# Handover from the up to the down projection: load order, glu stores, h in quarters, and turn 1's sums

## The reference, cut to what matters

```
h = x + hybrid_mixer(rms_norm(x, norm1_w), ...)
u = causal_dwconv(rms_norm(h, norm2_w) @ w_up, conv_w) + conv_b      # w_up: 1024 x 5632, 3 taps
gate, val = split(u, 2)
x = h + (silu(gate) * val) @ w_down                                  # w_down: 2816 x 1024
out = rms_norm(x, final_norm_w)
```

## Time and profile before

| | |
|---|---|
| median of 3 runs | 1639.51 us (1639.09 to 1640.14) |
| the profiled execution | 1641.98 us |
| its span | 1640.3 us, mean granted TensorE clock 0.993 |
| busy: TensorE matmul, VectorE, ScalarE, GpSimd | 1596.2, 882.6, 578.5, 648.6 us |
| TensorE's share of the chain that ended last | 91% |
| up projection from turn 1 | about 998 to 1408 us |
| down projection and final norm | about 1409 us to the end |

### The profile page before, as it was taken

The page is one execution under the profiler, slowest core; times in us unless marked ns, Lnnn a source line. Parts: engine busy times, 40 slices in busy tenths (PEclk is TensorE's granted clock), DMA queues, the critical chain, the costliest instruction groups (busy, mean ns, idle before and its releaser), DMA issues.

```text
span 1640.3 us, 20502 instructions
## 1 busy us (share of the span) xinstructions
PE 1596.2 (97%) x7955; PEld 1328.8 (81%) x7955; DVE 882.6 (54%) x1326; ACT 578.5 (35%) x838; POOL 648.6 (40%) x477
## 2 busy tenths in 40 slices
PE   7999999999999999999999998999999999889998
PEld 4888888888888888887888886888888888678886
DVE  5322223454536353567453248566665566678876
ACT  4422222123232234323222234444444444344445
POOL 3334332213132222224324357878888877000011
PEclk9999999999999999999999999999999999999999
DMA  5232432121213042444466022222333332696685
GB/s 170 70 97 79 122 89 60 42 72 34 69 38 86 20 125 76 129 109 140 141 209 224 37 93 71 90 91 92 111 112 116 104 103 78 206 336 207 196 265 183
DMA packets 202764, 192.24 MB, mean 117 GB/s; under 512 B 23236, under 2 KB 156844, under 8 KB 202668
## 3 DMA queue, kind: packets, MB, share of 16 engines
q1 hardware_dynamic: 202448, 190.85, 37.4%
q10 hardware_dynamic: 220, 0.09, 0.0%
HBM read 142.57 MB, written 48.33 MB: 116 GB/s over the span
## 4 chain that ended last, share of the span: by engine, by line
PE 91%; DVE 5%; DMA 2%; issue 1%; SPq 1%; ACT 0%; POOL 0%; DVEq 0%
PE acc L561 37%; PE acc L2449 12%; PE bank_ab L1407 7%; PE bank_ab L2449 6%; PE acc L2459 6%; PE att_ps L2449 5%; PE att_ps L2459 3%; PE bank_ab L2459 3%; PE acc L1842 3%; PE att_ps L1482 2%; PE bank_ab L1842 1%; PE att_ps L1842 1%; DMA f_raw<-in_w_down_dram 1%; PE att_ps L1464 1%; DVE u_t_full L1798 1%
## 5 line engine op out<-in xcount | busy, mean ns | idle before, releaser
L561 PE MATMUL acc<-xh,w_high 128*128 128x512 f32 x832 | 276.8, 409 | 0.6 <-POOL xl L1731 0.6
L561 PE MATMUL acc<-xl,w_high 128*128 128x512 f32 x832 | 262.2, 392 | 0.0
L561 PE MATMUL acc<-xh,w_low 128*128 128x512 f32 x832 | 261.1, 390 | 0.0
L972 POOL TENSOR_TENSOR w_low<-w_raw,w_high 128x1024 fp32r<-128x1024 f32 x49 | 117.4, 2396 | 347.3 <-ACT w_high L1054 347.3
L561 PEld LDWEIGHTS acc<-xh,w_low 128*128 128x128 f32 x832 | 156.5, 188 | 34.2
L561 PEld LDWEIGHTS acc<-xl,w_high 128*128 128x128 f32 x832 | 156.6, 188 | 33.9
L561 PEld LDWEIGHTS acc<-xh,w_high 128*128 128x128 f32 x832 | 147.1, 189 | 27.0 <-issue 3.8
L1145 ACT ACTIVATE sc<-sc,mx 128x128 f32<-128x128 f32 (+1 forms) x96 | 35.5, 440 | 173.5 <-DVE mx L1351 173.5
L1245 DVE SCALAR_TENSOR_TENSOR cs<-acc,prm,cs 128x1023 f32<-128x1023 f32 (+2 forms) x36 | 46.1, 1281 | 77.0 <-ACT cs L1072 76.1
L2236 POOL TENSOR_TENSOR f_h<-f_h,f_fw 128x512 f32<-128x512 f32 x8 | 11.0, 1369 | 184.8 <-ACT f_junk L2159 184.8
L2459 PE MATMUL acc<-f_w_high,f_gh 128*128 128x512 f32 x176 | 69.9, 397 | 12.2 <-DVE f_gl L2321 12.1
(11 more groups left out here) (386 smaller groups left out, 3831.6 us busy)
## 6 DMA issues: line engine op xcount, KB each, us to landing
w_raw<-in_w_in_dram SPq DMA_DIRECT2D x51, 512.0 KB, 4.5
f_raw<-glu_d SPq DMA_DIRECT2D x66, 256.0 KB, 3.0
f_raw<-in_w_down_dram SPq DMA_DIRECT2D x55, 256.0 KB, 3.8
w_raw<-in_w_up_dram SPq DMA_DIRECT2D x24, 512.0 KB, 5.1
glu_d<-u_free_high SPq DMA_DIRECT2D x22, 512.0 KB, 4.7
u_raw_even<-in_w_up_dram SPq DMA_DIRECT2D x20, 512.0 KB, 4.6
f_raw<-gsum_d SPq DMA_DIRECT2D x33, 256.0 KB, 3.3
conv_d<-so SPq DMA_DIRECT2D x16, 512.0 KB, 3.0
```

What stands on the lines that cost most here:

```text
L561: mm = nc.tensor.matmul(out[:, lo:hi], w, xx[:, lo:hi], start=first and j == 0, stop=last and j == 2)
L972: g.tensor_tensor(wl[:, n % 2], raw[:, n % 2], wh[:, n % 2].bitcast(F32), ALU.subtract).then_inc(s_wlo, 1)
```

## The change

- Room 0 of `f_raw` now lies where the even turns' raw weights lay (8 KB into the old room), so load 0 is issued in SP's pass for turn 20, behind that turn's `load_back`; `combine(0)`, whose target lies over a moving operand of turn 21, waits for turn 21's second product. Room 3 is cut into three pieces 8 KB apart; rooms 1 and 2 keep a piece of the old room each.
- The last glu store and glu sum store are issued behind load 12 in place of ahead of load 8.
- h is loaded in 16 quarters (4 row tiles by one 512-column half at a time, 256 KB each), one with each of steps 9 to 24, in place of 8 tiles of 512 KB with steps 8 to 15. Each `add` to a quarter waits for that quarter's four loads (the semaphores `rows_loaded`, which the first norm used for x, count on). `final_norm_w` follows at step 25 in place of 16.
- VectorE's turn 1 runs mix 0, 1, 2, `taps(0, 0)`, mix 3, `taps(0, 1)`, mix 4, `gated(0)`, mix 5, `glu_sum(0)`; before it ran `taps(0, 0)`, mix 0, `taps(0, 1)`, `gated(0)`, mix 1 to 3, `glu_sum(0)`, mix 4, mix 5.

```diff
@@ ffn: rooms @@
-    room = nc.alloc_sbuf_tensor_at("f_raw", [P, RING, 3, HALF], F32, offset=OL_AT)
+    slots = [nc.alloc_sbuf_tensor_at(f"f_raw{j}", [P, 3, HALF], F32, offset=at)
+             for j, at in enumerate((OL_AT + 8 * KB, OL_AT, OL_AT + 16 * KB))]
+    slots.append(nc.alloc_sbuf_tensor_at("f_raw3", [P, 3, 4 * HALF], F32, offset=OL_AT + 6 * KB))
...
     def slot(n):
-        return room[:, n % RING]
+        return slots[n % RING][:, :, 0:HALF]
@@ ffn: SP @@
                 if t >= KH:
                     load_back(t)
+                if t == LAST - 1:
+                    load(0)
 
             sp.wait_ge(s_prod, NP * (LAST - 1) + 3)
-            for n in range(NS):
-                if n == 2 * RING:
+            for n in range(1, NS):
+                load(n)
+                if n == KH + 1:
                     store_glu(LAST)
                     store_sum(LAST)
-                load(n)
-                if n == 2 * RING:
+                if n == KH - 2:
 
                     sp.wait_ge(s_prod, NP * LAST)
                     sp.wait_ge(s_mix, NP * LAST)
-                if 2 * RING <= n < 2 * RING + NT:
-                    st = n - 2 * RING
-                    sp.dma_start(h[st], halves(h_d[st * P:(st + 1) * P, :])).then_inc(s_h, 16)
-                if n == 2 * RING + NT:
+                if KH - 2 <= n < KH - 2 + 2 * NT:
+                    quarter, i = divmod(n - KH + 2, NTH)
+                    rows = slice((NTH * (quarter // 2) + i) * P, (NTH * (quarter // 2) + i + 1) * P)
+                    cols = slice(quarter % 2 * HALF, (quarter % 2 + 1) * HALF)
+                    sp.dma_start(result(i, HQ[quarter]), h_d[rows, cols]).then_inc(s_rows[quarter], 16)
+                if n == KH - 2 + 2 * NT:
@@ ffn: VectorE, combine @@
                     loaded(dve, n)
+                    if n == 0:
+
+                        dve.wait_ge(s_prod, NP * (LAST - 1) + 2)
@@ ffn: VectorE, add @@
                     to = result(i, name)
+                    if name in HQ:
+                        dve.wait_ge(s_rows[HQ.index(name)], 16 + 16 * NTH)
@@ ffn: VectorE, turns @@
             for t in range(1, FT):
-                if t > 1:
-                    mix(t - 1, 6)
+                if t == 1:
+
+                    for n in range(3):
+                        mix(t, n)
+                    taps(t - 1, 0)
+                    mix(t, 3)
+                    taps(t - 1, 1)
+                    mix(t, 4)
+                    gated(t - 1)
+                    mix(t, 5)
+                    glu_sum(t - 1)
+                    continue
+                mix(t - 1, 6)
                 taps(t - 1, 0)
-                if t == 1:
-                    mix(t, 0)
                 taps(t - 1, 1)
-                if t > 1:
-                    mix(t, 0)
+                mix(t, 0)
                 gated(t - 1)
...
                 if p and RING <= kk < RING + NTH:
-                    if p == 1 and kk == RING:
-                        dve.wait_ge(s_h, 16 * NT)
                     add(p - 1, kk - RING)
```

More of the change, by code:

```diff
@@ L240, in build @@
         m_ring, g_ring, u_ring = (ring_sems(phase) for phase in "mgu")
+        s_rows = [sem(f"rows_loaded{i}") for i in range(NT)]
         ups = UpRoom(nc, sem, xh, xh_at, xl, xl_at, ring, u_ring[0], nc.sbuf_base)
@@ L243, in build @@
               norm1_w, norm2_w, dn_conv_w, ffn_conv_w, ffn_conv_b, w_in2, dn_a_log, dn_dt_bias, dn_onorm_w, conv_d, og_d, ob_d, gate_d, m_d, t_d,
-              w_pa2, w_pb2, ring, m_ring, g_ring)
+              w_pa2, w_pb2, ring, m_ring, g_ring, s_rows)
         merged, merged_banks = merge_and_project(nc, sem, acc, every, ident, small, prm, xh, xl, w_pa2, w_pb2, w_o2, places, ready,
@@ L247, in build @@
         ffn(nc, sem, sb, mixed, merged, merged_banks, acc, bank_ab, att_ps, every, prm, small, xh, xl, w_up2, w_dn2, h_d, glu_d, gsum_d, final_norm_w,
-            outd, ring, u_ring, xl_at, ups)
+            outd, ring, u_ring, xl_at, ups, s_rows)
 class UpRoom:
@@ L385, in norm_head @@
 def norm_head(nc, sem, xd, norm1_w, norm2_w, dn_conv_w, ffn_conv_w, ffn_conv_b, ident, ones, prm, small,
-              xs, xn, junk, n1w, stage, tps, prm_ps, acc, xh, xl, w_in2, ring, m_ring):
+              xs, xn, junk, n1w, stage, tps, prm_ps, acc, xh, xl, w_in2, ring, m_ring, s_x):
     ss, ms, rstd, mhalf = small[:, 0:8], small[:, 8:16], small[:, 16:24], small[:, 24:32]
@@ L391, in norm_head @@
     first_cols = [job[2] for job in mixer_jobs()[0:2]]
-    s_x = [sem(f"n_x_loaded{i}") for i in range(NT)]
     s_par, s_n1w = sem("n_params_loaded"), sem("n_weight_loaded")
@@ L577, in mixer @@
           norm1_w, norm2_w, dn_conv_w, ffn_conv_w, ffn_conv_b, w_in2, dn_a_log, dn_dt_bias, dn_onorm_w, conv_d, og_d, ob_d, gate_d, m_d, t_d,
-          w_pa2, w_pb2, ring, m_ring, g_ring):
+          w_pa2, w_pb2, ring, m_ring, g_ring, s_rows):
     bank_a, bank_b = bank_ab[:, 0:HALF], bank_ab[:, HALF:S]
@@ L736, in mixer @@
             xs, xn, vt[:], n1w, stage, [att_ps[:, :], bank_ab[:, :]], acc[1][:, HALF:HALF + PT_COLS], acc,
-            xh, xl, w_in2, ring, m_ring)
+            xh, xl, w_in2, ring, m_ring, s_rows)
         A4 = bank_a[:, :].rearrange("p (h c) -> p h c", h=NH)
@@ L1918, in ffn @@
 def ffn(nc, sem, sb, mixed, merged, merged_banks, acc, bank_ab, att_ps, every, prm, small, xh, xl, w_up2, w_dn2, h_d, glu_d, gsum_d, final_norm_w,
-        outd, ring, u_ring, xl_at, ups):
+        outd, ring, u_ring, xl_at, ups, s_rows):
     raw, wh, wl = ring
@@ L1953, in ffn @@
     s_k, s_bank, s_sum = sem("f_k_done"), sem("f_bank_done"), sem("f_summed")
-    s_h, s_fw = sem("f_h_loaded"), sem("f_norm_loaded")
+    s_fw = sem("f_norm_loaded")
+    HQ = ("00", "01", "10", "11")
     s_sq, s_ms, s_rstd = sem("f_squares"), sem("f_mean_square"), sem("f_rstd")
```

## The result

The changed kernel takes 1626.64 us (median of 6 runs, 1624.81 to 1627.56) against 1639.6 us of 6 runs of the kernel before: 13.0 us less, ratio 0.9921, 95% interval 0.9908 to 0.9934. The profiled execution took 1627.18 us, its span is 1625.4 us, 14.9 less than before. Forecast were 1621.5 and a gain of 18.0: the time lies in the range, 5 us above the point.

What follows compares the result with a forecast made beforehand. TensorE was taken to carry the chain, so only its waits and low-clock time could be won. Handover 12.8 (15.7 less 0.7, 1.0, 1.2) plus turn 1 5.2 gave 18.0, off the median 1639.51: 1621.5 us, range 1617.0 to 1627.5.

Steps and rivals of the forecast that it cites:

- Part 1: Turn 1's sums ahead of turn 0's taps: 6.77 us late becomes a 1.6 wait for GpSimd, gain 5.2 (4.2 to 6.1).
- Part 2: Load 0 issued a turn earlier: load 1 lands at 1405.1, down projection starts without its 1.66 us gap.
- Part 3: VectorE's chain after combine 1: load 5's 2.16 us wait dropped, taps at 1416.0 on before's clock, step 6 loses 0.7.
- Part 4: Glu store later: loads 8 to 12 no longer queue behind it, the 8.1 us wait goes, step 7 loses 1.0.
- Part 5: New VectorE wait: combine 11 waits for both last stores, landing taken as 3.9 us, step 10 loses 1.2.
- Part 6: h in quarters with steps 9 to 24: same 4 MB, 16 issues, cost nothing, hidden under the steps.
- The starved case: Rival in the down projection: h transfers starve the sixteen steps from step 9, time 1644 us, chance 0.03.
- I take the 18.0 off the median: Whole kernel: the 18.0 us gain is subtracted from the runs' median of 1639.51, giving 1621.5.
- clock full throughout: Sign of being right, listed with turn 1's: TensorE's granted clock stays full; 0.50 in either place would show it wrong.
- no new waits: Rival, turn 1 and handover: faster loads, stores in 3.1, GpSimd undisturbed; at most 22.5 us gained, 1617.0, chance 0.15.
- the store wait's rival: At step 10 the store wait replaces the load wait: 5.0 + 2.1 in place of 1.2, 1627.4 us, chance 0.12.
- the others: Rivals: early load does nothing, 1623.8, chance 0.12; turn 1 stays slow, 1625, 0.08; transfers starve the steps, 1644, 0.03.

Runs made afterwards that it cites:

- a0: The changed kernel again, no edit, profiled and timed beside the kernel before; ratio 0.9926, span 1623.1 us.
- e4: The changed kernel with load 0 issued in its old place, behind the wait for turn 21's third product; ratio to before 0.9941.
- e5: The changed kernel with the quarters of h loaded with steps 13 to 28 in place of 9 to 24; ratio to before 0.9925.
- e6: The kernel before with only the last glu store and sum store moved behind load 12; ratio to before 0.9982.
- e8: e3 with turn 21's gating and glu sum moved behind step 7's low parts on VectorE; median 1622.01 us, ratio to before 0.9894.
- e0: The kernel before, profiled once more with no edit; span 1638.6 us, handover 425.00 us.
- e9: e8 with e7's edit added (mix 5 ahead of turn 0's gating); median 1622.31 us, ratio to before 0.9895.
- the seven named: Profiles of the new order with slow matmuls behind turn 1's wait (a0, e1, e3 and its repeat, e4, e8, e9); turn 1 34.3 to 34.4 us.
- e2: The changed kernel with turn 1's order on VectorE put back, so the handover part only; ratio to before 0.9962.
- the other three: Profiles of the new order without slow matmuls behind turn 1's wait (the changed kernel, e5, e7); turn 1 35.3 to 35.4 us.
- e7: The changed kernel with mix 5 ahead of turn 0's gating in turn 1; span 1624.8 us, no ratio.
- e1: The kernel before with only turn 1's order on VectorE changed; ratio to before 0.9979.
- e3: The changed kernel with the last glu store and sum store ahead of load 11 in place of behind load 12; ratio to before 0.9901.

## Why the prediction was right, and where its size was off

- *Part 1, turn 1.* Turn 2 was to start at 1021.7 and started at 1021.61, by low 0 as releaser; 5.23 against 5.2. That the wait for mix 1 would go and low 0 would be next is right; that the point was met so closely is partly luck. The added 0.9 is no share of each VectorE operation but a race: low 0 took 2.2 to 2.3 when the gating came first and 1.3 when it did not, and then there is no wait; a0, the same kernel, gained 6.2. The Trainium skill's exclusive port pair ("SBUF — State Buffer", "SBUF: two separate sides") describes that better than my half sum did.
- *Part 2, load 0.* TensorE started without a gap, and e4 shows that the early load brings 2 us. Load 1 came even earlier, combine 1 at 1398.43 where 1399.9 was said (1405.1 less the 5.2 of turn 1); later loads gave 1.2 of it back.
- *Part 3.* The taps were to start at 1410.8 and did at 1410.61; step 6 lost 0.6 against 0.7. The dropped wait for load 5 did not vanish (0.95), the earlier start paid for it.
- *Part 4.* Step 7 lost 0.95 against 1.0, behind combine 8 at 1421.09 (forecast 1421.4).
- *Part 5, the step that was off.* SP issued the sum store at 1426.27 (forecast 1426.7), but it landed after 5.7, not 3.9. Step 10 came 2.8 late, not 1.2, and the clock fell behind a wait of 2.53, which I had charged only to a wait of 5: step 10 took 4.34 in place of 2.72, another 1.6. Together 4.4 in place of 1.2, and that is nearly all of the difference between the handover's 9.5 and the 12.8 of the sum. The landing was late in a0 too (5.6, step 10 2.7 late), the low clock was not there, so the first half of the miss is the kernel's and the second belongs to the execution. I stayed close to a landing with little ahead of it; here loads 11 and 12, a quarter of h and the glu store stood ahead. e5 shows that such neighbours count (4.9 without h), e6 how far (7.1), and e8 that with 2 us of quiet ahead of the stores 3.4 is right.
- *A reading that was off.* Step 11 of before starts at 1453.20, not at 1453.36, where the chain's piece ends. The handover was 15.5 late, not 15.7, and the low clock behind the wait of 8.08 cost 1.9, not 2.1.
- *Part 6.* Quarters cost nothing on TensorE; no wait after step 10. The starved case did not come.
- *From span to median.* For the last 2 us (14.9 by spans, 13.0 by medians) the step "I take the 18.0 off the median" is to blame: the terms were made from one profiled execution that lay 2.4 above its median, that of the changed kernel lay 0.5 above its own, and e0 shows a handover 1.3 shorter in another profile of before. Which stretch is shorter in the median execution no profile shows.
- *The signs named ahead.* No wait of the sixth product, step 0 without a gap, and three short waits at steps 6, 7 and 10 came true. Combine 11 was released by the sum store, not the glu store. One sign of being wrong came true as well: the clock at 0.50 at step 10, over 1434 to 1436; in a0 it stayed full there and fell to 0.50 in turn 1 instead. So the forecast lies in its range while its "clock full throughout" did not hold.

The rivals: "no new waits" did not come true for this kernel (e9, with three more moves, comes to it in the handover); the store wait's rival was the one that the result leaned to, about halfway; the others did not occur.

## What to carry to other kernels

When a store is moved out of the way of loads, ask who waits for the store, and put it where the queue idles anyway: here no later load was waited for in TensorE's list, and it won 2.5 to 4 us. A landing is priced by a row with the same neighbours just ahead on the queue: 3.1 to 3.5 with nothing issued in the last 2 us, 5.3 to 5.7 directly behind loads and a quarter of h. Price a stall of a couple of us with the slow matmuls that may follow it, and read parts of a few us from stretches inside the profile, not from medians.

## What was not expected of the hardware

The granted clock fell behind a wait of 2.53 (changed) and of 1.79 (e5) at step 10, and stayed full behind 2.41 at the same step in a0. It fell behind the wait of 2.25 to 2.27 ahead of turn 1's third product in eight profiles (the seven named and e2), while in before, e0, e6 and the other three it stayed up. The length of a wait of about 2 us does not tell whether the clock falls. VectorE and GpSimd, each with two inputs from SBUF, ran nearly one after the other, and a lead of 0.02 (e7) to 0.10 us (e1, e3) was enough to decide the order.
